# Order of the merge's loads, the end of the experts' stage, and two of eight rows combined on TensorE

## The reference

```
ga, gb, gc = split(sigmoid(gate_cols), 3)              # gate_cols = h @ w_in's last 3072 columns
merged = ga * (ya @ w_branch[0]) + gb * (yb @ w_branch[1]) + gc * (yc @ w_branch[2])
x = x + gx1 * (merged @ w_out)
h2 = rms_norm(x, norm2_g) * (1 + scx2) + shx2
# 64 experts of width 128; each token goes to its best 8, weighted by normalised sigmoid scores
routed = einsum('tef,efd->td', silu(hg) * hu * gates[:, :, None], w_down)
x = x + gx2 * (routed + shared)
```

## Time and profile before

| | us |
|---|---|
| median of 3 runs (lowest to highest) | 3064.5 (3062.82 to 3071.03) |
| the profiled execution, its own time | 3067.44 |
| its span, first to last instruction | 3065.4 |
| merge of layer 0, first load to last addition | 913.95 to 1185.21 |
| merge of layer 1 | 2494.05 to 2636.89 |
| combination of layer 0, first load to last addition | 1673.20 to 1727.42 |
| combination of layer 1 | 3030.13 to 3060.16 |
| mean granted clock of TensorE over the span | 0.90 |

### The profile page before, as it was taken

The page is one execution under the profiler, slowest core; times in us unless marked ns, Lnnn a source line. Parts: engine busy times, 40 slices in busy tenths (PEclk is TensorE's granted clock), DMA queues, the critical chain, the costliest instruction groups (busy, mean ns, idle before and its releaser), DMA issues. The chain is left out here.

```text
span 3065.4 us, 49817 instructions
## 1 busy us (share of the span) xinstructions
PE 2499.0 (82%) x20220; PEld 1632.3 (53%) x20220; DVE 1255.5 (41%) x2753; ACT 799.4 (26%) x1915; POOL 465.8 (15%) x544
## 2 busy tenths in 40 slices
PE   7999898577769997899896399998577759787984
PEld 3444554466644444466664246475477648664542
DVE  4877656655551113532222600055655531332214
ACT  2101454433330002122221100154333330121220
POOL 0000001244400000032221000001244400121220
PEclk9999898798879997999998699998788889899997
DMA  8555011000005201599985623122000042199894
GB/s 344 225 229 210 28 39 48 15 3 3 3 23 231 83 0 45 230 382 360 348 321 206 266 82 110 55 64 77 2 3 3 3 174 94 59 392 366 352 360 190
DMA packets 72788, 461.99 MB, mean 151 GB/s; under 512 B 19056, under 2 KB 25328, under 8 KB 43376
## 3 DMA queue, kind: packets, MB, share of 16 engines
q1 hardware_dynamic: 45808, 408.42, 34.0%
q0 software_dynamic: 26752, 50.39, 4.3%
HBM read 441.95 MB, written 62.91 MB: 165 GB/s over the span
## 5 line engine op out<-in xcount | busy, mean ns | idle before, releaser
L501 PE MATMUL win_ps<-h,win_ring 128*128 128x512 f32 (+1 forms) x1024 | 396.8, 549 | 18.6 <-PEq L377 13.3
L2280 PE MATMUL xp_psG<-moe_ring,rt_xt 128*64 128x256 f32 (+1 forms) x2048 | 349.3, 395 | 6.5 <-DMA moe_ring<-in_moe 6.2
L501 PEld LDWEIGHTS win_ps<-h,win_ring 128*128 128x128 f32 x1024 | 195.8, 192 | 211.0 <-issue 204.2
L2280 PEld LDWEIGHTS xp_psG<-moe_ring,rt_xt 128*64 128x64 f32 (+1 forms) x2048 | 253.3, 166 | 77.3 <-issue 22.2
L561 DVE SCALAR_TENSOR_TENSOR mod_acc<-ada_ring,cv_silu,mod_acc 128x512 f32<-128x512 f32 x280 | 198.0, 748 | 10.8 <-issue 0.4
L2301 PE MATMUL xp_psY<-moe_ring,rt_aT 128*64 128x512 f32 (+1 forms) x512 | 179.1, 610 | 14.3 <-DVE rt_aT L2552 14.3
L2163 POOL DMA_INDIRECT y_rows<-rt_y,rt_dst x92 | 92.5, 1005 | 493.0 <-DVE rt_y L2557 249.9
L1896 PE MATMUL mg_psG<-h,mg_ring 128*128 128x512 f32 (+1 forms) x480 | 166.7, 507 | 0.0
L1696 PE MATMUL sc_ps<-sc_NT,sc_XI 64*64 64x64 f32 x2560 | 157.2, 227 | 1.0
L1696 PEld LDWEIGHTS sc_ps<-sc_NT,sc_XI 64*64 64x64 f32 x2560 | 146.3, 143 | 3.2 <-DVE sc_XI L1581 3.2
L2265 PEld LDWEIGHTS xp_psT<-cst,rt_xg 128*128 128x128 f32 x736 | 83.6, 143 | 111.2 <-DMA rt_xg<-h_rows,rt_tok 72.4
(11 more groups left out here) (444 smaller groups left out, 4196.2 us busy)
## 6 DMA issues: line engine op xcount, KB each, us to landing
moe_ring<-in_moe SPq DMA_DIRECT2D x128, 1536.0 KB
ada_ring<-in_ada SPq DMA_DIRECT2D x22, 2048.0 KB, 15.4
win_ring<-in_win SPq DMA_DIRECT2D x20, 2048.0 KB, 8.4
cb_yg<-y_rows SPq DMA_DIRECT2D x24, 1024.0 KB, 7.1
mg_ring<-in_mg SPq DMA_DIRECT2D x10, 1536.0 KB, 6.9
mg_ring<-in_mg SPq DMA_DIRECT2D x16, 768.0 KB, 5.3
ml_gate_ring<-in_mg SPq DMA_DIRECT2D x18, 512.0 KB, 3.6
mg_wo<-in_wo SPq DMA_DIRECT2D x2, 4096.0 KB, 26.1
```

Of the source, the lines that this page charges most:

```text
L501: last = pe.matmul(ps[:, n % NB, first(n):T], ring[:, j % 2, c, m * P:(m + 1) * P], h[:, c, first(n):T], start=c == 0, stop=c == KD - 1)
L2280: last = pe.matmul(psG[at:at + m, u % 2, 0:2 * P].rearrange("p (q n) -> p q n", q=2), xt[:, u % 2, c, at:at + m], ring[:, slot, c:2 * KD:K ...
```

## The change

It has three parts.

In the merge, SP issues the branch blocks of steps 2 and 3 ahead of most gate blocks, and the output matrix and the tokens later, behind the branch blocks of steps 4 and 5. Within a step the branch block now comes before the gate block, so a gate block stands behind the wait for branches(m-2) as well.

The blocks of the experts' stage and of the combination are opened with `no_gpsimd_drain=True`.

In the combination, `cb_yg` gets eight slots in place of four. VectorE multiplies and adds six of the eight rows; rows 2 and 5 go to TensorE, which multiplies them by a diagonal matrix with the tokens' weights and so turns, weighs and adds them in `cb_ps` at once. The turn of VectorE's sum becomes a product with the identity that adds to the same place. VectorE builds the diagonal matrices at the start (8 in layer 0, 4 in layer 1). The output is stored in two pieces; SP waits for the first to land before it goes on to the second.

```diff
-                load_gates(M0)
-                load_gates(M0 + 1)
-                sp.dma_start(wo[:], k.d_wo[l]).then_inc(wo_in.sem, 16)
-                sp.dma_start(x[:, :, t0:T], x_source[:, :, t0:T]).then_inc(x_in.sem, 16)
+                if M0 <= 2:
+                    load_gates(M0)
                 for m in range(2, KD):
+                    sp.wait_ge(y_done.sem, y_done.at(3 * (m - 1)))
+                    load_branch(m)
+                    if m == 2 and M0 > 2:
+                        load_gates(M0)
+                    if m == (2 if M0 <= 2 else 3):
+                        load_gates(M0 + 1)
                     if m >= M0 + 2:
                         sp.wait_ge(g_done.sem, g_done.at(3 * (m - 1) - A))
                         load_gates(m)
-                    sp.wait_ge(y_done.sem, y_done.at(3 * (m - 1)))
-                    load_branch(m)
+                    if m == 4:
+                        sp.dma_start(wo[:], k.d_wo[l]).then_inc(wo_in.sem, 16)
+                    if m == 5:
+                        sp.dma_start(x[:, :, t0:T], x_source[:, :, t0:T]).then_inc(x_in.sem, 16)
...
-        with nc.Block() as block:
+        with nc.Block(no_gpsimd_drain=True) as block:
...
-    SL, PER = 4, 2
+    SL, PER = 8, 2
+    BY_PE = (2, 5)
+    BY_DVE = tuple(j for j in range(TOP_K) if j not in BY_PE)
...
-                        sp.wait_ge(summed.sem, summed.at(PER * (m - SL + 1)))
-                    sp.dma_start(yg[:, m % SL], d_y[m // (NL // NTT), m % (NL // NTT)]).then_inc(y_in[m % SL].sem, 16)
+                        sp.wait_ge(summed.sem, summed.at(added(m - SL, BY_DVE)))
+                        sp.wait_ge(mixed.sem, mixed.at(added(m - SL, BY_PE)))
+                    sp.dma_start(yg[:, m % SL], d_y[m // NG, m % NG]).then_inc(y_in[m % SL].sem, 16)
                 if l == DEPTH - 1:
-                    sp.wait_ge(x_done.sem, x_done.at(NTT))
-                    sp.dma_start(k.d_out, x[:, :, CTX:T]).then_inc(out_done.sem, 16)
-                    sp.wait_ge(out_done.sem, out_done.at(16))
+                    for tt in range(NTT):
+                        sp.wait_ge(x_done.sem, x_done.at(tt + 1))
+                        sp.dma_start(k.d_out[:, :, tt * P:(tt + 1) * P], x[:, :, CTX + tt * P:CTX + (tt + 1) * P]
+                                     ).then_inc(out_done.sem, 16)
+                        sp.wait_ge(out_done.sem, out_done.at(16 * tt + 16))
...
                 for tt in range(NTT):
-                    pe.wait_ge(summed.sem, summed.at(8 * (tt + 1)))
                     if tt >= 2:
                         pe.wait_ge(x_done.sem, x_done.at(tt - 1))
+                    for i, j in enumerate(BY_PE):
+                        m = (tt * TOP_K + j) // PER
+                        pe.wait_ge(diag_done.sem, diag_done.at(tt * NP + i + 1))
+                        pe.wait_ge(y_in[m % SL].sem, y_in[m % SL].at(16 * (m // SL) + 16))
+                        for c in range(KD):
+
+                            last = pe.matmul(ps[:, tt % 2, c], yg[:, m % SL, j % PER, c * P:(c + 1) * P],
+                                             diag[:, tt * NP + i], start=i == 0 and c % 4 == 0, stop=False)
+                        last.then_inc(mixed.sem, 1)
+                    pe.wait_ge(summed.sem, summed.at(ND * (tt + 1)))
                     for c in range(KD):
-                        last = pe.transpose(ps[:, tt % 2, c], acc[:, tt % 2, c * P:(c + 1) * P], k.cst("ident"))
+                        last = pe.matmul(ps[:, tt % 2, c], acc[:, tt % 2, c * P:(c + 1) * P], k.cst("ident"),
+                                         start=False, stop=c % 4 == 3)
                     last.then_inc(turned.sem, 1)
```

More of the change, by code:

```diff
@@ L2600, in stage_combine, with added @@
     NTT = N // P
-    SL, PER = 4, 2
-    NL = NTT * TOP_K // PER
+    SL, PER = 8, 2
+    NG = TOP_K // PER
+    NL = NTT * NG
+    BY_PE = (2, 5)
+    BY_DVE = tuple(j for j in range(TOP_K) if j not in BY_PE)
+    ND, NP = len(BY_DVE), len(BY_PE)
     y_in = k.signals(*[f"cb_y{j}" for j in range(SL)])
-    summed, turned, x_done, out_done = k.signals("cb_summed", "cb_turned", "cb_x", "cb_out")
+    diag_done, summed, mixed, turned, x_done, out_done = k.signals(
+        "cb_diag", "cb_summed", "cb_mixed", "cb_turned", "cb_x", "cb_out")
+    def added(m, rows):
+        return (m // NG) * len(rows) + sum(j < PER * (m % NG + 1) for j in rows)
     with ExitStack() as ctx:
@@ L2607, in stage_combine @@
         acc = ctx.enter_context(nc.sbuf_tensor(f"cb_acc{l}", [P, 2, D], F32))
+        diag = ctx.enter_context(nc.sbuf_tensor(f"cb_diag{l}", [P, NTT * NP, P], F32))
         ps = ctx.enter_context(nc.psum_tensor(f"cb_ps{l}", [P, 2, KD, P], F32))
-        d_y = k.d_y.rearrange("(t p g j) n -> t g p j n", p=P, g=TOP_K // PER, j=PER)
-        with nc.Block() as block:
+        d_y = k.d_y.rearrange("(t p g j) n -> t g p j n", p=P, g=NG, j=PER)
+        with nc.Block(no_gpsimd_drain=True) as block:
             @block.sync
@@ L2636, in _ @@
                 for tt in range(NTT):
-                    for j in range(TOP_K):
+                    for i, j in enumerate(BY_PE):
+                        n = tt * TOP_K + j
+                        dve.tensor_scalar(diag[:, tt * NP + i], k.cst("ident"), gj[:, n:n + 1], None, ALU.mult
+                                          ).then_inc(diag_done.sem, 1)
+                for tt in range(NTT):
+                    for i, j in enumerate(BY_DVE):
                         n = tt * TOP_K + j
                         m = n // PER
-                        if j % PER == 0:
-                            dve.wait_ge(y_in[m % SL].sem, y_in[m % SL].at(16 * (m // SL) + 16))
+                        dve.wait_ge(y_in[m % SL].sem, y_in[m % SL].at(16 * (m // SL) + 16))
                         row = yg[:, m % SL, j % PER]
-                        if j == 0:
+                        if i == 0:
+                            if tt >= 2:
+                                dve.wait_ge(turned.sem, turned.at(tt - 1))
                             dve.tensor_scalar(acc[:, tt % 2], row, gj[:, n:n + 1], None, ALU.mult
@@ L2646, in _ @@
                         else:
-                            dve.wait_ge(summed.sem, summed.at(n))
+                            dve.wait_ge(summed.sem, summed.at(tt * ND + i))
                             dve.scalar_tensor_tensor(out=acc[:, tt % 2], in0=row, scalar=gj[:, n:n + 1],
@@ L2667, in stage_combine @@
             y_in[j].advance(16 * NL // SL)
-        for s, n in zip((summed, turned, x_done, out_done), (8 * NTT, NTT, NTT, 16 * (l == DEPTH - 1))):
+        for s, n in zip((diag_done, summed, mixed, turned, x_done, out_done),
+                        (NTT * NP, NTT * ND, NTT * NP, NTT, NTT, 16 * NTT * (l == DEPTH - 1))):
             s.advance(n)
```

## The result

The changed kernel takes 3041.5 us (median of 4 runs, 3036.2 to 3045.4), the kernel before 3066.6 in the same session (4 runs, 3062.8 to 3071.0). The ratio is 0.9912, with an interval of 0.9890 to 0.9934: 25 us or 0.9% faster. The forecast was 3025.5, range 3019 to 3035: right in its sign, 14 us too large in its gain (-39.0 against -25.0), and the time lies outside the range.

A forecast was written before the change was run, and what follows sets the result against it. A chain of stages that no work crosses was taken as the bound, so savings on a stage's chain count fully: -21.5 - 12.8 - 4.3 - 0.4 = -39.0 from 3067.4, 3028.4; 3025.5 us as a median, range 3019 to 3035.

The forecast's parts named there:

- Merge, layer 1: Merge of layer 1: branch block 2 no longer queues behind other loads, so gates(4) starts earlier; -21.5 us, bounds -15.5 and -22.2.
- Merge, layer 0: Merge of layer 0: gate matmuls wait 0.0 us, so nothing can be gained; 0 us.
- The drain at its own place: End of the experts' stage: gaps of 8.9 and 7.0 us shrink by 6.6 and 6.2, -12.8 us, bounds -15.3 and -8.
- three signs that were to refute the forecast: Gap after the experts stays at 7 us; TensorE idles nowhere in the combination; merge block 2 lands after 2515.
- Combination, layer 0: Combination of layer 0, four tiles: two rows leave VectorE, transfers pace at 9.9 us per tile; -4.3 us.
- the second rival: Combination, layer 0: the forecast's words for the lower bound on its -4.3 us; its numbered rival 2 concerns the experts' gap.
- the term of the unhidden turn: Combination, layer 0: the last turn takes 3.6 us, not hidden under the 2.15 us residual, so 50.7 us instead of 48.9.
- Layer 1 and output: Combination of layer 1 wins nothing; output in two serial pieces of 3.7 us; -0.4 us, bounds -3 and +1.8.
- Rival 1: Combination: TensorE at the low clock paces tiles, 10.6 to 11.1 us each; +3.4 and +0.8 us, total 3029.7; 25%.
- Rival 2: Gap after the experts: GpSimd's own waits, loop end and barrier, not the drain; 12.8 us not saved, 3038.3; 9%.
- rival 3: Combination: weight loads and fp32 products do not overlap; six tiles 50 to 110 us more, total 3080 to 3141; 2%.
- rival 4: Merge stalls again at block 2 or 3 behind unfinished loads; half of the 21.5 us kept, total 3036; 6%.

The follow-up runs named there:

- The line put back: The changed kernel with GpSimd's drain at the end of the combination's block restored, the experts' block still without: 0.9846 of the kernel before, 3019.3 us against 3067.8.
- the nearest relative of the kernel with both drains gone: The kernel before with only the experts' block opened without GpSimd's drain, the combination's drain kept: 0.9951 of the kernel before, -15 us.
- the drain timed: The changed kernel plus three one-column GpSimd memsets with two explicit drains between them, beside the combination's loads: 3031.7 us in one run.

## Why the prediction was wrong, point by point

**The step that failed** is the last sentence on the drain: "In the combination's own block the drain costs nothing now (0.27) and is worth nothing." The 0.27 us were read rightly, and two explanations fit them: the drain had nothing left to do, since the one at the experts' end had done it, or it ran hidden beside the loads. The first was true of the kernel before: a second drain takes 0.12 us. With the experts' drain gone the same instruction becomes the cover under which 9 us pass unseen, and it was worth all of the saving in layer 0. With it failed the premise that "each saving counts in full if it is on its own stage's chain": this wait crossed into another stage, 520 us later. I asked what takes the place of the drain at its own barrier, and not which drain GpSimd comes to next. The answer stood in the code: line 1516. For the merge I had asked what could be late next; for the drain I did not, because it was priced as an instruction and not as a debt.

**The size of it.** By the totals the second drain's removal costs 9 us: the kernel with only the experts' drain gone is 15 us under the kernel before, the one with both gone 6. The stand itself is 9.0 us. What it adds to the stage is less certain: with it the scan takes 394.2 to 394.8 us, without it 384.1 to 386.8 in the kernels with the new combination, 7 to 11 us less, but 378.9 in the nearest relative of the kernel with both drains gone, 15.9 less. In the profiled execution the places of the forecast and the scan make up -22.1 (merge) - 8.6 and - 6.8 (ends of the experts' stages) - 2.5 (combination, layer 0) - 0.2 (layer 1 and output) + 7.1 (scan) = -33.1, and the span shrank by 24.8: all the other stages together took 8.3 us more, in the second trace of the changed kernel 4.9. They are spread in pieces of up to 2 us in the one and 4.5 in the other, no experiment was aimed at them, and they are about as large as the interval of the result (7 us either side): that part of the missing 14 us stays open. The line put back gave 47 us (interval 37 to 58). The sum of 39.0 lies in that, but this does not prove the sum, since 7 us of the profiled gain lie in the scan of layer 0, where nothing was forecast.

**Merge, layer 1: right.** -21.5 forecast, -22.1 measured as the stage's length in the trace, -22 by the merge alone. The 0.2 us forecast for block 2 came out as 0, the 0.3 for block 3 as 0.79, and nothing was late behind them. **Merge, layer 0: right**, 0.9 us longer in this trace, and so in that of the kernel before built anew (293.1 against 292.2), so not the change's.

**The drain at its own place: right, and too cautious.** -12.8 forecast, the gaps shrank by 8.3 + 6.7 = 15.0. Nearly the whole gap was the drain: of the 2.3 us that I left in layer 0 for the instruction fetch 0.6 are there, the 0.3 of the barrier included. Of the three signs that were to refute the forecast none appeared, because all of them watched the places that the diff touches.

**Combination, layer 0: mechanism right, a size off.** -4.3 forecast (the middle of -5.3 and -3.5 is -4.4; and the bound that the text calls the second rival is the first). The last pair of rows was there at 43.6 us after the first load, where 41.9 was forecast, and the whole was 51.5 in place of 49.9: -2.7 in this trace. By the length from the first row load to the next stage's first loads it is -2.5 to -3.9 in five traces with this combination. The first rows landed where forecast (4.85 us); by their pace of 421 GB/s the last pair would have been there 1.4 us earlier than it was, and why it came late is open. The last residual waits 1.02 us for the turn, which took 3.00 us at a granted clock of 0.66 (window 1717.50 to 1720.60); at full clock a turn took 2.05. In the traces with the line put back and with the drain timed the last turn took 2.05, nothing waited for it, and the stage was 51.5 us to the next stage's store in place of 52.9. So the term of the unhidden turn was real and depended on where the clock fell. **Layer 1 and output: right.** -0.4 forecast, -0.2 measured (35.3 to 35.1 us); the sum had both ends too early, 34.9 and 34.5. Two pieces of 512 KB took 7.6 us together, 3.8 each where I took 3.7. The Trainium skill's page "DMA: Bandwidth & Descriptors", section "Anatomy of one DMA — SWDGE (gpsimd) path", would give an estimated 3.2, by a fit to transfers that GpSimd issues; SP issues these, and the trace shows 3.5 as the median from issue to landing, a little more.

**Rival 1 (TensorE at the low clock) fell as a pace, not as a clock.** The granted clock was 0.50 until the first rows had landed and 0.62 while TensorE worked through its first 32 records, which took 6.47 us, 0.20 each. From 1686 to 1711.30 it was 0.94 on average, although TensorE stood 0.3 to 3.1 us between its pieces, and sixteen records took 2.02 or 2.05 us, 0.13 each, not 0.22. Yet two of the four turns ran slower, behind pauses of 3.08 and 2.64 us: 3.32 us at 1707.69, where the clock was 0.59, and 3.00 at 1717.58; another behind a pause of 3.08 us, at 1696.28, took 2.05. Neither made TensorE the pace, since it went on waiting for rows or for VectorE's sums. The Trainium skill's page "TensorE: Matmul & The Clock Gate", section "HAM oscillation — how this bites in real kernels", has bursts of matmuls between DMA waits start cold each time; the trace shows it for the first piece and for two turns that waited for VectorE, not each time. **Rival 2 (the gap is not the drain) fell** by the timed drain, **rival 3 (products that don't overlap) fell** with the same 0.13 us, **rival 4 (the merge stalls again)** is the 0.79 us. What happened was none of the four.

## What to carry to other kernels

GpSimd's drain was a debt here, not a cost: taking it out moved the wait to the next drain on the same engine. Before such an instruction is dropped, look for the next one and ask what it lies on; the best place for it is a stretch where that engine has nothing to do and the stage is paced by something else, as here 50 us of loads. And when the parts of a change, measured alone, add up to more than the whole, look for the part whose saving another part was hiding, by comparing the lengths of all stages and not just of those in the diff. Take two traces of one kernel first, to see which lengths repeat.

## What the runs showed of the hardware

- GpSimd's first drain after a series of indirect transfers takes long, though they have all landed (VectorE's copies at the experts' end wait for that): 8.96 us after layer 0's 104 transfers (52 gathers, 52 scatters), 7.01 after layer 1's 80. It is as long after 520 us of other stages, 8.99 at line 1516, as at once. A second drain takes 0.12. The two points are 1.95 us apart for 24 transfers, 0.08 us each; whether the price goes by their number was not tested.
- The scan of layer 1, the same code with no stand in it, took from 378.1 to 388.5 us in nine programs, but came out 0.03 us apart in two executions of one program (with the stand 0.04). The granted clock over 130 us of it, from 120 us after its first load, is 0.89 in the one with 378.1 and 0.83 in the kernel before. Which part of a change moves it was not found.
